# Second block's first projection started from the uncentred sum, with its rotary tables built on GpSimd

## The reference, cut to what matters

```python
def layer_norm(x, g, b):
    mu = jnp.mean(xf, axis=-1, keepdims=True)
    var = jnp.mean(jnp.square(xf - mu), axis=-1, keepdims=True)
    y = (xf - mu) * lax.rsqrt(var + LN_EPS) * g + b
...
# first block, layers 0 (hybrid) and 1 (MLA)
    f = jnp.square(jax.nn.relu(h @ mlp_w1[i])) @ mlp_w2[i]
    e = jax.nn.sigmoid(h @ ple_w_gate[i]) * (p[i] @ ple_w_proj[i])
    x = layer_norm(DN_ALPHA * h + f + e, ln2_g[i], ln2_b[i])
...
# second block, each layer
    mod = jax.nn.silu(c) @ w_ada + b_ada
    h = modulate(rms_norm_2(x, norm1_g), shift1, scale1)
    p = h @ w_in
    y_rwkv = rwkv7_time_mix(p[..., RET_COLS:RET_COLS + RWKV_COLS], ...)   # tanh(wd) @ w_lora comes first
    q = rotary(q, positions)
```

## Time and profile before

| | us |
|---|---|
| median of three executions | 2345.61 |
| lowest and highest of them | 2345.43, 2345.95 |
| profiled execution | 2345.03 |
| its span in the trace | 2343.2 |
| TensorE busy in the span | 2214.6 |
| VectorE busy | 983.8 |
| ScalarE busy | 465.2 |
| GpSimd busy | 310.7 |

### The profile page before, as it was taken

One profiled execution on the slowest core, in us unless ns is written; L12 is line 12 of the kernel. 1 busy time (PEld: TensorE's weight loads), 2 busy tenths in 40 slices (PEclk: granted clock), 3 DMA queues, 4 the chain that ended last, 5 costly groups with the idle time before them and its releaser, 6 DMA issues.

```text
span 2343.2 us, 33634 instructions
## 1 busy us (share of the span) xinstructions
PE 2214.6 (95%) x14454; PEld 1522.4 (65%) x14454; DVE 983.8 (42%) x1816; ACT 465.2 (20%) x1065; POOL 310.7 (13%) x259
## 2 busy tenths in 40 slices
PE   9999999999999999999888888899999999888887
PEld 8777777687768899997333333388999863333333
DVE  5588855468866666532100000055755230000001
ACT  3422213522214321312000000033113020000001
POOL 2300002210003055500000000012454000000000
PEclk9999999999999999999999999999999999999999
DMA  7287752278752433359999999944243799999998
GB/s 281 98 330 281 284 185 92 102 278 303 301 198 81 139 122 122 109 217 409 427 428 428 428 427 428 412 172 147 91 145 109 308 415 428 427 428 428 428 428 316
DMA packets 136864, 654.93 MB, mean 279 GB/s; under 512 B 9865, under 2 KB 15113, under 8 KB 108169
## 3 DMA queue, kind: packets, MB, share of 16 engines
q1 hardware_dynamic: 136712, 652.72, 70.2%
HBM read 651.64 MB, written 1.05 MB: 279 GB/s over the span
## 4 chain that ended last, share of the span: by engine, by line
PE 74%; DMA 20%; DVE 2%; ACT 2%; SPq 1%; issue 1%; POOL 0%; DVEq 0%; ACTq 0%; POOLq 0%
PE bank L853 73%; DMA ring<-in_w_exp_up 12%; DMA PRGT<-in_w_exp_up 4%; DMA ring<-in_w_exp_down 1%; DMA ring<-in_w_exp_gate 1%; DMA PRGT<-in_w_exp_down 1%; SPq L767 1%; ACT R L3651 1%; PE bank L1544 1%; DVE sm L2302 0%; POOL PRGT L3751 0%; ACT SQ L3693 0%; PE bank L1039 0%; DVE PRGT L2854 0%; ACT PRGT L3462 0%
## 5 line engine op out<-in xcount | busy, mean ns | idle before, releaser
L853 PE MATMUL bank<-hT,ring 128*128 128x256 f32 (+1 forms) x2288 | 402.7, 330 | 0.0
L853 PEld LDWEIGHTS bank<-hT,ring 128*128 128x128 f32 x2288 | 357.9, 191 | 62.4 <-issue 14.4
L853 PE MATMUL bank<-PRGT,R 128*32 128x512 f32 (+1 forms) x1152 | 281.6, 598 | 31.3 <-DMA PRGT<-in_w_exp_up 15.3
L853 PE MATMUL bank<-ring,R 128*32 128x512 f32 (+1 forms) x992 | 256.7, 593 | 40.0 <-DMA ring<-in_w_exp_up 25.2
L853 PE MATMUL bank<-PRGT,ring 128*128 128x256 f32 (+6 forms) x1520 | 254.4, 354 | 1.2 <-ACT PRGT L3181 0.8
L853 PEld LDWEIGHTS bank<-PRGT,ring 128*128 128x128 f32 (+3 forms) x1520 | 214.1, 177 | 35.1 <-issue 4.2
L853 PE MATMUL bank<-PRGT,SQ 128*32 128x512 f32 (+2 forms) x864 | 192.9, 531 | 14.1 <-ACT SQ L3693 12.2
L853 PEld LDWEIGHTS bank<-PRGT,R 128*32 128x32 f32 (+1 forms) x1152 | 77.8, 114 | 195.5 <-issue 195.0
L853 PEld LDWEIGHTS bank<-ring,R 128*32 128x32 f32 (+1 forms) x992 | 70.5, 115 | 169.7 <-issue 168.8
L853 PE MATMUL bank<-ring,SQ 128*32 128x512 f32 (+2 forms) x640 | 163.6, 519 | 8.7 <-ACT SQ L3693 8.3
L853 PE MATMUL bank<-PRGT 64*64 64x64 f32 (+3 forms) x1584 | 145.4, 263 | 4.5 <-issue 1.7
(11 more groups left out here) (483 smaller groups left out, 2803.1 us busy)
## 6 DMA issues: line engine op xcount, KB each, us to landing
PRGT<-in_w_exp_gate SPq DMA_DIRECT2D x42, 2048.0 KB, 31.9
ring<-in_w_exp_up SPq DMA_DIRECT2D x36, 2048.0 KB, 32.0
ring<-in_mlp_w SPq DMA_DIRECT2D x32, 2048.0 KB, 9.6
PRGT<-in_w_exp_down SPq DMA_DIRECT2D x30, 2048.0 KB, 30.9
PRGT<-in_w_exp_up SPq DMA_DIRECT2D x28, 2048.0 KB, 31.8
PRGT<-in_w_ada SPq DMA_DIRECT2D x32, 1536.0 KB, 8.9
ring<-in_w_exp_down SPq DMA_DIRECT2D x24, 2048.0 KB, 33.6
ring<-in_w_exp_gate SPq DMA_DIRECT2D x22, 2048.0 KB, 32.0
```

The lines of the kernel that those rows point to most:

```text
L853: return mm(o, lhsT=lhsT, rhs=rhs, start=first, stop=last, **kw)
```

## The change

Seven edits, all in those two passages. First: in both layers ScalarE squares the third pair ahead of the last gate. Second: the twelve transposes of the modulation row go to `acc[0]`, `acc[1]` and one bank of `ada_t`, and the three idle products are left out; VectorE reads the three in one go, behind one wait. Third, in layer 1 alone: `AHEAD` is `R` with its mean still in it, times the gain, written by ScalarE between its gates and squares, and by VectorE (two tiles) ahead of the layer norm; a third extra column holds the gain, so that the product also gives the gain's own projection. Fourth: the first five row tiles of the product (`block_first(0, 5)`) stand right behind the transposes. Fifth: VectorE keeps minus the mean (`MINUS_MEAN`), and takes the four column tiles out of PSUM behind the second norm's scaling: one pass adds minus the mean times the gain's projection, one multiplies by the inverse deviation; the other two passes of `first_tiles` stay. Sixth: GpSimd takes the mean off `R` only when `AHEAD` is written. Seventh: the rotary tables are built on GpSimd, ahead of its sums in layer 1, from 24 operations of 128x256.

```diff
-                  ... (f"ada_t{_l}", 3)]
+                  ... (f"ada_t{_l}", 1)]
...
+            def block_first(k0, k1):
+                n, W = BANK_AT["first0"], slot(2, KT)
...
+                    pe.wait_ge(sems["ahead_in"], KT + k + 1)
+                    for c in range(4):
+                        if k == 0:
+                            pe.wait_ge(bank_read[(n + c) % BANKS], emptied(n + c))
+                        ins = mul(bk(n + c)[:, 0:S + 3], W[:, k, c * P:(c + 1) * P], AHEAD[:, k, :], k == 0, k == KT - 1)
...
-                idle_products(acc[0], 3)
+                if l:
+                    block_first(0, FIRST_TILES)
...
                 else:
-                    first_two_pairs(0, 5, range(4))
                     rms_norm()
-                    for j in range(2):
-                        first_two_pairs(5, KT, (2 * j, 2 * j + 1))
+                    block_first(FIRST_TILES, KT)
...
                 def modulation():
+                    if l:
+                        v.tensor_scalar(MINUS_MEAN, stat[:, 0, :], -1.0, None, ALU.mult)
+                    dve.wait_ge(bank_full[t0 % BANKS], filled(t0))
                     for q in range(3):
...
+                if l:
+                    dve.wait_ge(sems["ahead_in"], KT * l + ACT_AHEAD)
+                    for m in range(ACT_AHEAD, KT):
+                        v.tensor_scalar(AHEAD[:, m, 0:S], R[:, m, :], gain[:, m:m + 1], None, ALU.mult).then_inc(sems["ahead_in"], 1)
+                layer_norm(l == 0, modulation, None if l else ahead)
...
                 if l == 0:
-                    rotary_tables()
                     dve.wait_ge(sems["norm_out"], L.nxt("norm_out", KT))
                 rms_norm(xT[:, :, :], hT[:, :, :], KT, l)
+                if l == 0:
+                    for c in range(4):
+                        dve.wait_ge(bank_full[(n0 + c) % BANKS], filled(n0 + c))
+                        ins = v.tensor_copy(at(c), bk(n0 + c)[:, S:S + 3])
+                    stepped(ins)
+                    for c in range(4):
+                        v.scalar_tensor_tensor(PR[:, 28 + c, :], MINUS_MEAN, at(c)[:, 2:3], bk(n0 + c)[:, 0:S], ALU.mult, ALU.add).then_inc(
+                            bank_read[(n0 + c) % BANKS], 1)
+                    for c in range(4):
+                        dve.wait_ge(bank_read[(n0 + c) % BANKS], filled(n0 + c))
+                        ins = v.tensor_tensor(PR[:, 28 + c, :], PR[:, 28 + c, :], stat[:, 1, :], ALU.mult)
+                    stepped(ins)
...
                 gate(0)
+                gate(1)
                 for j in range(3):
-                    gate(j + 1)
                     square(j)
+                    if l:
+                        ahead(2 * j, 2 * j + 1)
+                    if j == 1:
+                        gate(2)
+                gate(3)
                 ada_row(0)
                 square(3)
...
+            def rotary_tables():
+                pool.wait_ge(sems["p_loaded"], 16 * (DEPTH + 1))
+                ang, turns, part = POOL_CD[:, 78, :], POOL_CD[:, 79, :], pT[:, 0, :]
+                chained(nc.gpsimd.tensor_copy(ang, posi[:, :]))
+                chained(nc.gpsimd.tensor_scalar(ang, ang, C("inv_freq"), None, ALU.mult))
+                for dst, shift in ((sinT, 0.0), (cosT, 0.25)):
+                    chained(nc.gpsimd.tensor_scalar(turns, ang, 1.0 / (2 * math.pi), shift, ALU.mult, ALU.add))
...
+                    if r and mixer == "mla_out":
+                        rotary_tables()
...
+                    if r and mixer == "mla_out":
+                        pool.wait_ge(sems["ahead_in"], 2 * KT)
                     center(sq)
```

More of the change, by code:

```diff
@@ L3365, in ada_row, with ahead, centred_ahead @@
                     copy_out(BANK_AT[f"ada{l}"] + q, ADA_ROW[:, q * 512:(q + 1) * 512])
+                gain = sm[:, AG:AG + KT] if l else V_("ln2_g0")
+                def ahead(*tiles):
+                    for k in tiles:
+                        f(AHEAD[:, k, 0:S], R[:, k, :], ACT.Copy, scale=gain[:, k:k + 1]).then_inc(sems["ahead_in"], 1)
+                def centred_ahead():
+                    for j in range(ACT_AHEAD // 2):
+                        act.wait_ge(sems["norm_centered"], 8 * l + 4 + j + 1)
+                        ahead(2 * j, 2 * j + 1)
                 gate(0)
+                gate(1)
                 for j in range(3):
-                    gate(j + 1)
                     square(j)
+                    if l:
+                        ahead(2 * j, 2 * j + 1)
+                    if j == 1:
+                        gate(2)
+                gate(3)
                 ada_row(0)
@@ L3373, in ffn_and_ple @@
                 ada_row(2)
[L3375 to L3383, removed]
+                layer_norm(xT, f"ln2_g{l}", f"ln2_b{l}", beside=None if l else centred_ahead)
             attention(4, 0, DSA_D ** -0.5, 4)
@@ L3762, in center @@
                     nc.gpsimd.tensor_tensor(both(q, R), both(q, R), bcast(stat[:, 0, :], 2), ALU.subtract).then_inc(sems["norm_centered"], 1)
+            def rotary_tables():
[5 more added lines that the diff above has]
+                    chained(nc.gpsimd.tensor_scalar(turns, ang, 1.0 / (2 * math.pi), shift, ALU.mult, ALU.add))
+                    chained(nc.gpsimd.tensor_scalar(turns, turns, 12582912.0, None, ALU.add))
+                    chained(nc.gpsimd.tensor_scalar(turns, turns, -12582912.0, None, ALU.add))
+                    for i, step in enumerate(TWO_PI):
+                        chained(nc.gpsimd.tensor_scalar(part, turns, -step, None, ALU.mult))
+                        chained(nc.gpsimd.tensor_tensor(dst[:, :], dst[:, :] if i else ang, part, ALU.add))
+                    chained(nc.gpsimd.tensor_scalar(dst[:, :], dst[:, :], shift * 2 * math.pi, 3.1415925, ALU.add, ALU.min))
+                    nc.gpsimd.tensor_scalar(dst[:, :], dst[:, :], -3.1415925, None, ALU.max).then_inc(sems["rot_in"], 1)
             def norms(mixer):
@@ L3767, in norms @@
                 i0 = L.nxt("norm_in", 4) - 4
-                for ready in (lambda q: (bank_read[(m0 + q) % BANKS], filled(m0 + q)), lambda q: (sems["norm_in"], i0 + q + 1)):
+                for r, ready in enumerate((lambda q: (bank_read[(m0 + q) % BANKS], filled(m0 + q)), lambda q: (sems["norm_in"], i0 + q + 1))):
+                    if r and mixer == "mla_out":
+                        rotary_tables()
                     sq = L.nxt("norm_sq", 4) - 4
```

82 lines of the change are left out of this document (26 added, 56 removed).

## The result

The changed kernel takes **2349.27 us** (median of 22 runs, 2345.48 to 2352.04) against 2345.43 (median of 22 runs of the kernel before, 2344.88 to 2346.74). The ratio is 1.0015, with an interval of 1.0008 to 1.0021: 3.8 us slower, where 0.9 us faster was forecast. The difference is real and lies outside the predicted range, 2343.2 to 2346.8, but under the 4.7 us named as the bound of "no change".

The account below looks back on a forecast made before the run. TensorE's own work was taken as the bound (74% of the span), with only its idle time in two passages to win. -0.84 (layer 0) and -0.05 (layer 1) make -0.89 us: 2344.7 against the median, range 2343.2 to 2346.8.

Parts of the forecast that it names:

- the sum: Whole kernel: layer 0 at -0.84 us and layer 1 at -0.05 us give -0.89 us.
- The third square: Both layers: squaring before the last gate removes TensorE's 0.84 us gap ahead of the norm's sums; layer 0 gains 0.84 us.
- The projection's start: Layer 1: earlier projection, broken after six loads for `MINUS_MEAN`; its 40 loads end 1.9 us earlier, bounds 1.2 to 2.6.
- The tables: Layer 1: rotary tables hidden on GpSimd, 684.5 to 703.5; the second inverse on VectorE starts 0.80 us earlier.
- The way out: Layer 1: VectorE's column tiles take 3.46 us, 2.65 more; the lora products wait 2.4 us, handing back the projection's gain.
- The clock: Rival, lora products in layer 1: TensorE's clock falls in the 2.4 us wait, costing 1.55 us, giving 2346.3; chance 0.12.

Follow-up runs that it names:

- the kernel of the last experiment: Changed kernel with column tiles 2 and 3 and the wait for all of `hT` behind `mix`, and `MINUS_MEAN` behind the three additions: 2343.34 us, ratio 0.999.
- the delay in the kernel before: Kernel before with three unused 128x512 products on VectorE behind the first two column tiles, making `mix` late: 2350.67 us, ratio 1.002.
- the filled kernel: Changed kernel with five idle products of 128x256 on TensorE ahead of the lora products: 2346.26 us, ratio 1.0004.

## Why the prediction was wrong, point by point

Behind the sum stands a start of the lora products 0.89 earlier than before; they started 0.95 later. And behind them came a cost that the forecast had as a rival, at 0.12, and too small.

**The third square: the step that failed first.** "The gap of 0.84 us goes" read the idle time of the weight loads as idle time of TensorE, which is how the text ahead of the prediction says that gaps are best read. The products' row covers it, and the square alone left it where it was. So both terms of -0.84 were nothing: in layer 0 the projection starts at 361.04, 0.09 later than before, and in layer 1 the sums' load comes at 722.44, which less the 0.36 of the next point is where it was. Leaving out the idle products in layer 0 cost nothing that can be seen: the wait that they filled lies bare now (1.31 ahead of the load at 361.04), and the 64 loads behind it take 13.73, before 13.77.

**A cost that wasn't in the sum.** All of layer 1 is 0.36 late already when it begins (the modulation row's products start at 719.73, before at 719.37). The rows at 435.91 and 439.67 show where it arises: in the MLA attention VectorE's masking operation waits 0.45 for the one before it, GpSimd's scaling follows late, and TensorE's transposes have 0.53 idle ahead of them instead of 0.17. Every kernel with the changed banks of the modulation row shows it there, and neither of the two that change only the square or the tables does. The banks are handed out in turn, and the change takes two fewer in each layer, so that the attention meets its banks shifted; that this is the cause was argued, not tried.

**The projection's start** came out at -1.34: the sums' loads of the second norm start at 736.41 - 0.36 = 736.05, where they started at 737.39 in the kernel before. The forecast was -1.9, of which 0.84 was the square's. The rest held, in order: six loads, a break, and 34 loads in 7.29. `MINUS_MEAN` took 1.36 beside GpSimd's centring (the forecast gave it 1.28), where the same form took 0.78. Less the 0.36 it ended at 728.43, 0.83 later than forecast, which is the square's 0.84; 0.3 of that came back, mostly because TensorE resumed 0.06 behind the additions and not 0.28.

What sets such a duration can be read from the traces: in the kernel after, the centring operation of GpSimd beside `MINUS_MEAN` ran from 727.32 to 728.63, and `MINUS_MEAN` ended 0.16 behind it, at 728.79. Other operations of its form and size in this passage that ran beside GpSimd end likewise some 0.15 behind a GpSimd operation: in the kernel before the one of 0.78 (727.16, GpSimd 727.00) and the table's at 735.18 (736.19, GpSimd 736.04), in the kernel of the last experiment `MINUS_MEAN` itself (728.66, GpSimd 728.51). With GpSimd idle the table's operation took 0.29 at 739.25 instead of 1.01. So 0.78, 1.01 and 1.36 aren't prices of the operation but what was left of GpSimd's when it started, and a forecast has to say beside which operation of GpSimd it falls. This agrees with the Trainium skill ("SBUF — State Buffer", section "Who interferes with whom"), by which the one that comes second waits for the other's end; no run here took GpSimd's centring away, so the shared ports as the reason are the skill's and not shown.

**The tables** were hidden, as forecast. GpSimd's 24 operations ran from 684.45 to 706.25, 21.8 us where 19 were estimated, nearly 6 us ahead of the sums. The second inverse follows the root directly (740.34 + 0.47, then 740.91), and 0.70 of the 0.80 was won.

**The way out** took 3.42 (747.24 to 750.66), forecast 3.46. Less the 0.36, VectorE starts it 2.03 earlier than before and it is 2.61 longer: 0.58 later, and the lora products came 0.59 later. The wait was 2.44, forecast 2.4; both of its ends came some 0.6 later than forecast (less the 0.36), since both hang on the projection's start. Here the sum held to a few hundredths, and the mechanism that decided the change (the gain ahead is handed back at the lora products) was the one forecast.

**The clock: the step that failed last and cost most.** The rival had the right place and the right wait, but the wrong size. It took the price from one stretch of 5 us behind a wait for a transfer (0.31 x 5 = 1.55), where the clock was back by 1274. Here it stayed at 1.2 GHz for 10 us, past the end of any one stretch of 5 us, and the price was about 4.8 us in this execution and 3.0 in the median.

The chance was read from two rows by the length of the wait alone, as a ladder on which 2.4 lies between 2.16 kept and 2.73 lost. But the row at 1152.16 above shows that the first was a single wait of 2.38 between products, after which the clock held, and here one of 2.07 brought it down; 2.4 was the wait of the loads, which the forecast set against waits of the products. And the two rows weren't all there was: the trace of the kernel before has 21 waits of the products of over 2 us, from 2.37 to 3.50. Behind 13 of them the granted clock of the next 4 us was 0.57 to 0.66 in the mean, behind eight it was 1.00, and waits of the same 2.73 stand on both sides (it held from 2240.08 on and was down behind 2249.87, the windows above). So the length of the wait alone doesn't order the cases, and counted over the trace the clock falls more often than not: two rows of another stage were no ground for 0.12. The Trainium skill's sentence that the forecast set against itself ("TensorE: Matmul & The Clock Gate", section "What's actually happening"), that the lower level is the default to which an idle TensorE returns, agrees with the kernel after and with the delay in the kernel before; in layer 0 the bare wait of 1.31, and in the experts eight of the 21 longer ones, left the clock where it was. That the 17 longer of the 22 times are those in which the clock fell fits the sizes (the first group lies where the filled kernel does), but only one of these executions has a trace, and it is one of the 17.

**The sum, with what the runs showed:** 2345.03 + 0.36 + 0.59 = 2345.98 for the profiled execution with the clock held; the filled kernel's profiled execution took 2345.86. With the clock: 2345.98 + 4.8 = 2350.8, and 2351.21 was measured. By the median of the filled kernel, 0.8 of the 3.8 us are work and 3.0 are clock; 0.8 is too little for its interval to tell from nothing, and rests on the trace.

## What to carry to other kernels

An idle time between weight loads is TensorE's only if the products' row has the same gap; look at both before you count on winning it. A change that shortens one chain and leaves TensorE waiting longer at the next join is not neutral: price the wait by its own length and by all of the time at the lower clock that follows it, and either fill it with idle products or shorten it. Of work that is moved in front of a join, move only what the next consumer needs: here two of four column tiles, which took back the 3.8 us; whether it wins anything on the kernel before isn't settled by the times.

## What the runs showed of the hardware

- Waits of 2.44 and 2.49 us (in the loads) ahead of the lora products, in two kernels, were followed in the traced execution of each by the clock's lower level for about 10 and 7 us. In the first the clock fell about when the wait ended (754.4), in the second about 1 us later (756.4 against 755.5). In the kernel after TensorE had been at 1.00 and busy in all of the 7 us before, and had work in hand at once when the wait ended. A wait of 0.85 there, and the longer waits filled with five products, left it at 1.00; so did 1.31 in layer 0. In the kernel before, eight of 21 waits of 2.37 to 3.50 between products left it at 1.00 and 13 did not. What besides the length decides, no run shows.
- While it was low, TensorE worked on the lora products, 16 of whose 24 loads are of 64 rows; it was back some 1.5 us after the large products of `hT` began (763.17) in the kernel after, and in the other kernel about when they began (763.28). Behind the wait at 1270.22 in the experts it was back by 1274. Whether the kind of work has to do with how long it stays low is open.
- GpSimd's prices in fp32 for 128x256, of which the forecast had only 0.686 for a product of two tensors. They depend on the form: the multiply-and-add with two constants was the cheapest (0.404), the addition followed by a minimum the dearest (1.076) but for the one cast from int32 (1.39, at 684.45 above). These are two of its groups of the table code in the kernel after (count, then busy us and mean ns, then idle time before):

```profile
L3768 POOL TENSOR_SCALAR PRGT<-PRGT 128x256 f32<-128x256 f32 x2 | 0.8, 404 | 0.2
...
L3774 POOL TENSOR_SCALAR pin<-pin 128x256 f32<-128x256 f32 x2 | 2.2, 1076 | 0.2
```
